# Order of work between latents, expansions, attention and pages in a one-core decoder layer: one change and its time

## The reference

```python
z = h @ lp["w_in"]
c_q, c_kv, k_pe, u = jnp.split(z, [Q_LORA, Q_LORA + KV_LORA, Q_LORA + KV_LORA + ROPE_DIM], axis=-1)
c_q = rms_norm(c_q, lp["q_lora_norm"])
q = (c_q @ lp["w_uq"]).reshape(*c_q.shape[:-1], N_HEADS, NOPE_DIM + ROPE_DIM)
q_nope = rms_norm(q[..., :NOPE_DIM], lp["q_nope_norm"])
q_pe = apply_rope(rms_norm(q[..., NOPE_DIM:], lp["q_pe_norm"]), cos[:, None], sin[:, None])
c_kv = rms_norm(c_kv, lp["kv_norm"])
k_nope = rms_norm((c_kv @ lp["w_uk"]).reshape(*c_kv.shape[:-1], N_HEADS, NOPE_DIM), lp["k_nope_norm"])
v = (c_kv @ lp["w_uv"]).reshape(*c_kv.shape[:-1], N_HEADS, V_HEAD)
# convolution: a causal depthwise window of 31 taps over 512 channels, for prompt and samples
y = lax.conv_general_dilated(xc, lp["conv_w"][:, None, :], (1,), "VALID",
                             dimension_numbers=("NWC", "WIO", "NWC"), feature_group_count=CONV_CH) + lp["conv_b"]
```

## Time and profile before

| what | value |
|---|---|
| median of 3 runs | 1878.46 us (1874.77 to 1879.05) |
| the profiled execution | 1870.42 us |
| its span | 1868.6 us |
| PE busy | 1764.5 us, 94% |
| DVE, ACT, POOL busy | 55%, 28%, 21% |
| mean TensorE clock granted | 0.987 of full speed |

### The profile page before, as it was taken

How to read it: one execution, slowest core, us unless ns; L and a number is a source line. 1 busy time by engine, 2 the same in 40 slices (tenths; PEclk the granted TensorE clock), 3 DMA queues, 4 the chain that set the end, 5 groups by cost and what they waited for, 6 DMA issues and landing times.

```text
span 1868.6 us, 27160 instructions
## 1 busy us (share of the span) xinstructions
PE 1764.5 (94%) x10268; PEld 1558.1 (83%) x10268; DVE 1021.3 (55%) x1659; ACT 529.8 (28%) x1040; POOL 385.6 (21%) x262
## 2 busy tenths in 40 slices
PE   7999798999898999879999999999999999999998
PEld 6999686667887887758788998998998998988886
DVE  5476885545988788766544334344244244244543
ACT  5212255655443444544421111111111111112211
POOL 2205594221545544432210000000000000000000
PEclk9999899999999999999999999999999999999999
DMA  6301000011411222220021111111111111112011
GB/s 197 113 8 40 10 1 1 1 36 37 131 52 52 60 58 56 61 97 1 1 68 46 46 45 45 45 45 45 45 45 45 45 45 45 45 68 76 29 43 41
DMA packets 108947, 91.89 MB, mean 49 GB/s; under 512 B 25571, under 2 KB 97792, under 8 KB 108845
## 3 DMA queue, kind: packets, MB, share of 16 engines
q1 hardware_dynamic: 106851, 89.63, 15.9%
q10 hardware_dynamic: 2002, 1.03, 0.2%
HBM read 84.73 MB, written 6.26 MB: 49 GB/s over the span
## 4 chain that ended last, share of the span: by engine, by line
PE 75%; DVE 12%; POOL 7%; ACT 3%; issue 2%; DMA 1%; ACTq 0%; DVEq 0%; SPq 0%; POOLq 0%
PE ps L1928 21%; PE ps L1930 21%; PE ps L1929 21%; DVE arena L1401 4%; POOL arena L881 2%; POOL stats L750 2%; PE ps L2342 2%; PE ps L2172 2%; DVE arena L1755 2%; PE ps L535 1%; PE ps L1935 1%; PE ps L2129 1%; POOL arena L793 1%; DVE arena L1627 1%; ACT prob_s L1092 1%
## 5 line engine op out<-in xcount | busy, mean ns | idle before, releaser
L1928 PE MATMUL ps<-h_hi,w_hi 128*128 128x384 f32 (+1 forms) x1056 | 345.6, 327 | 2.9 <-POOL h_lo L876 2.9
L1929 PE MATMUL ps<-h_lo,w_hi 128*128 128x384 f32 (+1 forms) x1056 | 345.4, 327 | 0.0
L1930 PE MATMUL ps<-h_hi,w_lo 128*128 128x384 f32 (+1 forms) x1056 | 345.4, 327 | 0.0
L1850 DVE TENSOR_TENSOR gate_s<-gate_s,ps 128x384 f32<-128x384 f32 (+1 forms) x66 | 35.1, 532 | 332.9 <-PE ps L1930 332.9
L881 POOL TENSOR_TENSOR arena<-arena,mhalf 128x32 f32<-128x32 f32 x32 | 173.7, 5429 | 167.5 <-DVE arena L1776 167.5
L1928 PEld LDWEIGHTS ps<-h_hi,w_hi 128*128 128x128 f32 x1056 | 198.5, 188 | 3.4 <-issue 3.1
L1929 PEld LDWEIGHTS ps<-h_lo,w_hi 128*128 128x128 f32 x1056 | 198.5, 188 | 0.5
L1930 PEld LDWEIGHTS ps<-h_hi,w_lo 128*128 128x128 f32 x1056 | 198.5, 188 | 0.0
L1862 DVE TENSOR_TENSOR arena<-arena,ps 128x512 f32<-128x512 f32 x187 | 128.4, 687 | 123.8 <-PE ps L1930 109.6
L529 POOL TENSOR_TENSOR stats<-stats,mhalf 128x1 f32<-128x1 f32 (+1 forms) x18 | 9.8, 543 | 883.1 <-DVE stats L519 883.1
L1928 PE MATMUL ps<-cw_hi,pT_hi 128*128 128x288 f32 x512 | 161.8, 316 | 6.6 <-DVE pT_lo L1674 5.0
(11 more groups left out here) (324 smaller groups left out, 3572.5 us busy)
## 6 DMA issues: line engine op xcount, KB each, us to landing
arena<-in_cache_ckv SPq DMA_DIRECT2D x128, 128.0 KB, 2.0
w_raw<-in_w_gate SPq DMA_DIRECT2D x22, 512.0 KB, 4.0
w_raw<-in_w_up SPq DMA_DIRECT2D x22, 512.0 KB, 5.2
arena<-in_x_prompt SPq DMA_DIRECT2D x16, 512.0 KB, 5.4
w_uk<-in_w_down SPq DMA_DIRECT2D x11, 512.0 KB, 3.5
w_uv<-in_w_down SPq DMA_DIRECT2D x11, 512.0 KB, 4.2
gw_raw<-in_w_in SPq DMA_DIRECT2D x8, 512.0 KB, 6.0
w_out<-in_w_out SPq DMA_DIRECT2D x1, 4096.0 KB, 13.3
```

The source lines that it names most:

```text
L1850: ch.link(nc.vector.tensor_tensor(gate_s[:, c], gate_s[:, c], ps[:, 2 * b + 1, 0:n], ALU.mult))
L1928: mm(out, left[0], right[0], start=start, stop=False)
L1929: mm(out, left[0], right[1], start=False, stop=False)
L1930: return mm(out, left[1], right[0], start=False, stop=stop)
```

## The change

- In the latents: the last latent tile goes to banks 0 and 1, and the squares of the last two tiles use banks 4 and 5 as scratch. ACT makes the high part of the key weights ahead of `high_c(NT-2)`, DVE the low part ahead of `latents(NT-1)`; the value weights' parts and the last tile's `high_c` and `low_c` move behind the first tile's squares and sums of the expansion. DVE makes no taps in the last latent step.
- On PE: the first keys wait for the squares of the last latent tile, no longer for its latents; `turn_c(NT-1)` stands behind the first keys; the values of tile 1 stand ahead of the first `turn_qk`.
- The samples' products: POOL makes two in latent step 4 and none in steps 7 and 8, so the latent loop makes 0 to 6 where it made 0 to 7; POOL's loop over the tiles of the expansion makes 7 to 15, product 7+i in tile i. DVE's loop there is unchanged.
- Taps: 2 fewer in the latents, 16 in the attention (4 behind the last wide copy of each pair of heads), 61 in place of 75 in the pages, there from page 7 of each sequence.

```diff
@@ -552,7 +552,7 @@
             return 4 if i == 0 else 0
         X_BANK = [0, 4] + [0] * (NT - 2)
         CONST_BANK, GOUT_BANK, CT_BANK, QT_BANK, Q_BANK, K_BANK, V_BANK, KT_BANK = 6, 6, 6, 0, 2, 4, 5, 6
-        Z_BANK = [4 - 2 * (t % 2) for t in range(NT)]
+        Z_BANK = [4 - 2 * (t % 2) for t in range(TILES)] + [0]
         GLU_BANK = [2 + 2 * (j % 3) for j in range(NU)]
         block = ctx.enter_context(nc.Block())
 
@@ -804,15 +804,17 @@
             pool.wait_ge(s_("hist_ready"), 2)
             for i in range(1, NT):
                 stat_z(i)
-                taps_sample(i - 1)
+                if i <= 4:
+                    taps_sample(i - 1)
+                if 4 <= i <= 6:
+                    taps_sample(i)
                 if i == 3:
                     pool.wait_ge(s_("w_high"), W_HIGH("wq"))
                     nc.gpsimd.tensor_tensor(wq_lo_r, wq_raw, wq_hi, ALU.subtract).then_inc(s_("w_low_pool"), 1)
             for i in range(NT):
                 stat_qk(i)
                 k_rope(i)
-                if i < 4 * CCH - (NT - 1):
-                    taps_sample(NT - 1 + i)
+                taps_sample(NT - 2 + i)
 
             pool.wait_ge(s_("khr_ready"), NT)
             pool.wait_ge(s_("qkv_done"), QKV(TILES, 3))
@@ -821,6 +823,7 @@
                 ch.link(nc.gpsimd.memset(pages[s][:, :, KL:KL + 1], 1.0))
                 nc.gpsimd.memset(pages[s][:, NPAGE, 0:KL], 0.0).then_inc(s_("page_set"), 1)
                 pool.wait_ge(s_("page_set"), s + 1)
+            pool.wait_ge(s_("ys_prod"), 4 * CCH)
             nc.gpsimd.memset(s_self[64:P, :, :, :], NEG).then_inc(s_("self_place"), 1)
             pool.wait_ge(s_("self_place"), 1)
             pool.wait_ge(s_("lat_stored"), 2 * NT * 16)
@@ -993,9 +996,12 @@
                     act.wait_ge(s_("row_sumsq"), NT + i)
                 else:
                     act.wait_ge(s_("hist_ready"), 1)
-                nc.scalar.activation(ps[0:r, 0, 0:QL], ps[0:r, b, 0:QL], ACT.Square, accum_out=st(z)[0:r])
-                nc.scalar.activation(ps[0:r, 1, 0:KL], ps[0:r, b + 1, 0:KL], ACT.Square, accum_out=st(z + 1)[0:r])
-                nc.scalar.activation(ps[0:r, 1, KL:KL + DR], ps[0:r, b + 1, KL:KL + DR], ACT.Square,
+                if i == NT - 2:
+                    act.wait_ge(s_("lat_ready"), i)
+                d = 0 if i < NT - 2 else 4
+                nc.scalar.activation(ps[0:r, d, 0:QL], ps[0:r, b, 0:QL], ACT.Square, accum_out=st(z)[0:r])
+                nc.scalar.activation(ps[0:r, d + 1, 0:KL], ps[0:r, b + 1, 0:KL], ACT.Square, accum_out=st(z + 1)[0:r])
+                nc.scalar.activation(ps[0:r, d + 1, KL:KL + DR], ps[0:r, b + 1, KL:KL + DR], ACT.Square,
                                      accum_out=st(z + 2)[0:r]).then_inc(s_("row_sumsq"), 1)
 
             def high_c(i):
@@ -1005,6 +1011,10 @@
                     src = ps[:, CT_BANK + b, 0:(k1 - k0) * P].rearrange("p (k c) -> p k c", c=P)[:, :, 0:r]
                     last = nc.scalar.activation(cT_hi_r[:, k0:k1, t * P:t * P + r], src, ACT.Copy)
                 last.then_inc(s_("act_high"), 1)
+            def high_kv(hi, w):
+                for k in range(LC):
+                    last = nc.scalar.activation(hi[k], w[:, k, :], ACT.Copy)
+                last.then_inc(s_("w_high"), 1)
             square_z(0)
             act.wait_ge(s_("glu_ready"), NU)
             nc.scalar.activation(glu_s[:, :, :, HIST:HIST + TQ], glu_new.rearrange("p c (b q) -> p c b q", q=TQ), ACT.Copy)\
@@ -1016,18 +1026,13 @@
                 square_z(t)
                 if t == 1:
                     act.wait_ge(s_("unit_done"), NU)
+                if t == NT - 1:
+                    act.wait_ge(s_("wkv_loaded"), 32)
+                    high_kv(wk_hi_r, w_uk)
                 high_c(t - 1)
                 if t == 3:
                     act.wait_ge(s_("wq_loaded"), 16)
                     nc.scalar.activation(wq_hi_r, wq_raw, ACT.Copy).then_inc(s_("w_high"), 1)
-
-            act.wait_ge(s_("z_done"), NT)
-            act.wait_ge(s_("wkv_loaded"), 32)
-            for hi, w in ((wk_hi_r, w_uk), (wv_hi_r, w_uv)):
-                for k in range(LC):
-                    last = nc.scalar.activation(hi[k], w[:, k, :], ACT.Copy)
-                last.then_inc(s_("w_high"), 1)
-            high_c(NT - 1)
 
             def square_qk(i):
                 r = rows_of(SEQ_TILES[i])
@@ -1062,6 +1067,9 @@
             for i in range(NT):
                 square_qk(i)
                 copy_qk(i)
+                if i == 0:
+                    high_kv(wv_hi_r, w_uv)
+                    high_c(NT - 1)
                 if i >= 1:
                     act.wait_ge(s_("qkv_done"), QKV(i, 3))
                     nc.scalar.activation(V[:, SEQ_TILES[i], :], ps[:, V_BANK, :], ACT.Copy).then_inc(s_("v_ready"), 1)
@@ -1497,22 +1505,25 @@
             ch.link(nc.vector.tensor_tensor(gq_col[0:DN, :], gq_col[0:DN, :], gk_col[0:DN, :], ALU.mult))
             ch.link(nc.vector.tensor_scalar(gq_col[0:DN, :], gq_col[0:DN, :], SCALE, None, ALU.mult))
             ch.link(nc.vector.tensor_scalar(g_qpe[:, :], g_qpe[:, :], SCALE, None, ALU.mult))
+            def low_kv(hi, lo, w, name):
+                dve.wait_ge(s_("w_high"), W_HIGH(name))
+                for k in range(LC):
+                    last = nc.vector.tensor_tensor(lo[k], w[:, k, :], hi[k], ALU.subtract)
+                last.then_inc(s_("w_low_dve"), 1)
             taps(2)
             latents(0)
             taps(2)
             for i in range(1, NT):
+                if i == NT - 1:
+                    low_kv(wk_hi, wk_lo_r, w_uk, "wk")
                 latents(i)
                 low_c(i - 1)
-                if i >= 2:
-                    sum_sample(i - 2)
-                taps(2)
-
-            for hi, lo, w, name in ((wk_hi, wk_lo_r, w_uk, "wk"), (wv_hi, wv_lo_r, w_uv, "wv")):
-                dve.wait_ge(s_("w_high"), W_HIGH(name))
-                for k in range(LC):
-                    last = nc.vector.tensor_tensor(lo[k], w[:, k, :], hi[k], ALU.subtract)
-                last.then_inc(s_("w_low_dve"), 1)
-            low_c(NT - 1)
+                if 2 <= i < NT - 1:
+                    sum_sample(i - 2 + (i > 4))
+                if i < NT - 1:
+                    taps(2)
+                if i == 4:
+                    sum_sample(3)
 
             def sums_q(i):
                 r = slice(0, rows_of(SEQ_TILES[i]))
@@ -1556,6 +1567,8 @@
             dve.wait_ge(s_("z_done"), NT)
             sums_q(0)
             sums_k(0)
+            low_kv(wv_hi, wv_lo_r, w_uv, "wv")
+            low_c(NT - 1)
             for i in range(NT):
                 if i >= 1:
                     qT_copy(i - 1)
@@ -1609,6 +1622,7 @@
                 if k >= 1:
                     wide_copy(k - 1)
                 if first:
+                    taps(4)
                     out_rows(2 * (k // TILES) - 2)
                 if k + 1 < STEPS:
                     row_max(0, k + 1)
@@ -1756,7 +1771,7 @@
                         .then_inc(s_("ksum_done"), 1)
                     if prev and g == 4:
                         row_of_max(b - 1, 1 - s)
-                    if g >= (4 if b == 0 else 6 - b % 2):
+                    if g >= 7:
                         taps(1)
                     if b == NSEQ - 1:
                         if g in WO_PAGE.values():
@@ -2077,18 +2092,20 @@
             for i in range(NT):
                 expand_q(i)
                 if i == 0:
-                    turn_c(NT - 1)
-                    pe.wait_ge(s_("lat_ready"), NT)
+                    pe.wait_ge(s_("row_sumsq"), 2 * NT)
                     pe.wait_ge(s_("w_low_dve"), 6)
                 else:
                     pe.wait_ge(s_("qk_copied"), 2 * i)
                 expand_kv(i, K_BANK, wk_hi_r, wk_lo_r)
-                if i >= 1:
+                if i == 0:
+                    turn_c(NT - 1)
+                if i == 1:
+                    pe.wait_ge(s_("w_low_dve"), 7)
+                    expand_kv(i, V_BANK, wv_hi_r, wv_lo_r)
                     turn_qk(i - 1)
-                    if i == 1:
-                        pe.wait_ge(s_("w_low_dve"), 7)
-                    else:
-                        pe.wait_ge(s_("v_ready"), i - 1)
+                if i >= 2:
+                    turn_qk(i - 1)
+                    pe.wait_ge(s_("v_ready"), i - 1)
                     expand_kv(i, V_BANK, wv_hi_r, wv_lo_r)
```

## The result

| | before | after |
|---|---|---|
| median | 1878.76 us (1874.77 to 1879.4, 4 runs) | 1905.09 us (1897.98 to 1909.43, 4 runs) |
| profiled execution | 1870.42, span 1868.6 | 1897.98, span 1896.1 |

The change makes the kernel slower: the ratio is 1.0141, 95% interval 1.0106 to 1.0176. The forecast was 1904.6. Further down, one execution of c_product_between (3009 us) and two of the kernel before (2000 and 3836 us) are left out of ranges and ratios. The two profiled spans differ by 27.5 us.

What follows compares the result with a forecast made beforehand. POOL was full in the expansion, paced at 8.2 us a tile by query statistic, scaling and sums. Terms +32.0, +1.7, 0 and −7.5 gave +26.2: 1896.6, by the median's level 1904.6 us; range 1890 to 1918.

Steps and rivals of the forecast that it cites:

- The products' order: Expansion: DVE waits for POOL's product of the same tile; pace 12.9 us a tile, 4.7 more than 8.21.
- the 12.9 and the 13.4 of the prediction: Expansion pace in us a tile: 12.9 if DVE and POOL no longer stretch each other's instructions, 13.4 if they do.
- The boundary: Latents to expansion: work taken out ahead of the first sums brings the first query statistic from 216.61 to 211.0, gain 5.6.
- The nine tiles: Expansion: from 211.0, tiles at 12.9 us end the last scaling at 325.65 instead of 293.65, +32.0 us.
- The clock at the attention's start: Last turns and scores before the attention: PE runs at a low clock after its idle hole, +1.7 us.
- my last term: Whole kernel: 8.04 us added for the median of the runs lying above the profiled execution.
- The taps in the attention: Attention: sixteen taps, four per pair of heads at 5.1 us, hide in DVE's idle 6.20 us; cost 0.
- the other end: Attention: POOL's splits stretch taps to 1.7 us each, overrunning by 0.6 four times, 2.4 us in all.
- The pages: Page stage: fewer, later taps save 4.3 on the last chunk's wait, 1.7 of clock and 1.5 elsewhere; −7.5 us.
- The dip that I let go with it: Page stage: the low PE clock following the last tap's wait goes too, saving 1.7 us.
- The rivals: Whole kernel: PE slows too (0.10); wait doesn't bite (0.05); loop takes only the 0.9 reduction (0.04); attention taps overrun (0.06).
- rival 1: Expansion: PE slows to at most 15.7 us a tile and sets the pace; 1924 us, likelier 1914; chance 0.10.

Runs made afterwards that it cites:

- c_product_between: Kernel after, with POOL's product of each tile moved between the query statistic and the key statistic; 1879.86 us, ratio 1.0018 to the kernel before.
- a_sum_later: Kernel after, with DVE reducing each samples' product of the expansion a tile later, behind the scaling; 1864.3 us, ratio 0.9926 to the kernel before.
- b_products_only: Kernel before, with only the order of the samples' products and their reductions changed as in the change; 1915.84 us, ratio 1.0205.
- e_boundary_only: Kernel before, with only the boundary changed (last latent tile's banks, key weights split first, turn behind first keys); 1877.74 us, ratio 0.9995.
- d_taps_only: Kernel before, with only the taps moved: four per pair of heads in the attention, the pages' taps from page 7; 1870.97 us, ratio 0.9964.
- d_taps_early_pages: Kernel before, with four taps per pair in the attention, the pages' taps still from page 4, 5 or 6; 1865.25 us, ratio 0.9946.
- f_fill_a: a_sum_later plus twelve unread PE transposes ahead of the last query turns; 1861.73 us, ratio 0.993 to the kernel before.
- f_fill_before: Kernel before plus twelve unread PE transposes ahead of the last query turns; 1876.8 us, ratio 0.9998.
- h_early: a_sum_later with the pages' taps back at page 4, 5 or 6 on; 1860.62 us, ratio 0.9918 to the kernel before.
- h_early_fill: h_early plus twelve unread PE transposes ahead of the last query turns; 1858.33 us, ratio 0.99 to the kernel before.
- h_early_again: h_early unchanged, run once more for the spread of its runs; 1860.44 us, ratio 0.9925 to the kernel before.
- t_six_taps: a_sum_later with six taps instead of four per pair of heads in the attention; 1869.91 us, ratio 0.9959 to the kernel before.

## Why the prediction was right, point by point

The pieces of all profiled executions, in us, carry this part:

| kernel | first statistic | expansions | attention's start | pairs 1 to 4 | pages | rest |
|---|---|---|---|---|---|---|
| before | 216.6 | 77.0 | 43.6 | 106.4 | 377.7 | 1047.2 |
| after | 209.5 | 111.4 | 47.8 | 107.8 | 370.8 | 1048.8 |
| a_sum_later | 210.9 | 75.4 | 53.8 | 107.9 | 373.6 | 1050.5 |
| b_products_only | 215.2 | 111.3 | 50.8 | 109.4 | 379.6 | 1050.3 |
| e_boundary_only | 214.4 | 75.4 | 49.0 | 109.4 | 379.2 | 1050.4 |
| d_taps_only | 216.2 | 74.3 | 51.6 | 107.9 | 369.3 | 1050.3 |
| d_taps_early_pages | 215.0 | 74.4 | 43.9 | 107.8 | 367.3 | 1050.5 |
| c_product_between | 209.7 | 88.8 | 50.6 | 109.3 | 369.8 | 1050.4 |
| f_fill_a | 210.3 | 75.2 | 44.2 | 106.4 | 369.8 | 1050.4 |
| f_fill_before | 215.7 | 74.4 | 47.3 | 109.4 | 379.6 | 1050.4 |
| h_early | 210.7 | 75.3 | 47.1 | 107.9 | 366.2 | 1050.4 |
| h_early_fill | 209.2 | 75.0 | 44.6 | 109.4 | 366.5 | 1050.3 |
| h_early_again | 209.4 | 74.9 | 51.1 | 106.4 | 366.1 | 1050.4 |
| t_six_taps | 210.3 | 75.3 | 47.1 | 121.5 | 367.0 | 1048.9 |

- **The products' order**: right, in mechanism and nearly in size. The pace is 12.51 instead of 12.9. POOL idles 4.8 us a tile, as forecast (about 5); DVE's wait for the product is 5.5 on average, where I had said some 4. Of the terms, POOL's whole tile is 7.72 (I took 7.9), the reduction 0.86 (0.93), the scaling 2.85 (2.9), sums with hops 1.08 (1.2). Each was a little high. For POOL's tile I had counted out only the 0.32 of L760; its copy of the rotary key fell as well, from 0.50 to 0.40, and L759 and L793 by some 0.05 each. What decides between the 12.9 and the 13.4 of the prediction is that the stretched forms went: with DVE idle POOL's L760 on 8 columns takes 0.24 and not 0.56, and with POOL idle DVE's last rotation takes 0.28 and not 0.48. With this the rule of the Trainium skill, page "SBUF — State Buffer", section "Who interferes with whom", agrees.
- **The boundary**: right. The first statistic came at 209.50, not 211.0, but 1.15 of these 1.5 us are the head start of this execution. Counted from DVE's taps of tile 4 the gain is 5.96, where I forecast 5.6. By the same count the seven other kernels with the whole boundary have 35.03 to 35.05 us up to the first statistic, and the three with the old latents and boundary 40.96 to 40.99, as before, so this measure repeats well. The push by the extra product at tile 4 was there: POOL's statistic of tile 5 came 3.3 later by this count, DVE's latents of tile 5 2.3 later and the last latents 1.5 later (I had 3.4, 2.4 and 1.9).
- **The nine tiles**: the last scaling ended at 320.88, not 325.65, +27.2 instead of +32.0. The 4.8 are 2.1 by the second tile's sums (221.5 instead of 223.6: 1.5 by the first statistic and 0.6 in the first tile, 0.4 of them on POOL) and seven tiles of 0.39.
- **The clock at the attention's start** (+1.7): this term failed. It measured +4.2, and the runs give its reason no support. A fixed dip added to a clean stretch can't be told: the column "attention's start" runs from 43.6 to 53.8 us over kernels in which that stretch holds the same work, and the profiled execution of before was the lowest of all. The 4.2 is a difference between two single executions, well inside that spread; what the change itself adds there stays open. That profile also had the lowest rest, 1047.2, and the lowest value between pairs 1 and 4, 106.4; on the other hand its expansions, 77.0, were 1.6 to 2.7 us above those of every kernel with that loop, the dip of the earlier trace rows. Such differences between executions are what my last term, 8.04 for the level of the median, stood for, and it did its work: the medians' difference, 26.3, is near that of the profiles, 27.5.
- **The taps in the attention** (0): right, by luck in its reason. I compared 5.1 us with the 6.20 of idle time and set the other end at 1.7 a tap. Two of the four places have POOL's splits beside them and the taps took 7.32, or 1.83 each: past that end. They were hidden all the same, because the earlier trace rows shows a hole up to the row scaling, and the deadline is later, at PE's next need of it. From the kernel before alone, the 1.97 us that DVE idles behind the scaling could have been added to the 6.20.
- **The pages** (−7.5): right, −6.9 between the two profiles. The last tap's wait went as said (5.1 to 0.8); the waits at the rotary turns gave 2.3 and those at the products 0.5, where I had 1.5 for both. The dip that I let go with it (1.7) came back elsewhere: over the last sequence, 806 to 848 us, the granted clock was 0.92, where before it was 1.00 over 782 to 822. Alone, the taps gave 6.6 us. I had counted three places where PE waits for DVE and missed the largest, 11.8 at L2332; it stayed (12.1), so the sum did not suffer.
- **The rivals**: none came. PE's clock fell often in its holes (0.88 over the 58 us, 0.75 to 0.91 tile by tile), but the pace stayed at 12.51 to 12.54: the slow stretches found room in PE's holes, the reason for which I gave rival 1 only 0.10.

That the sum came out within 0.5 us of the median is luck: errors of opposite sign met, −4.8 in the expansions with the boundary, and +2.5, +1.4, +0.6 and +1.6 in the terms behind them. The method was good to some 5 us, not to 0.5.

## What to carry to other kernels

Where a product is made at the end of one engine's step and consumed ahead of another engine's critical work, one step of distance hides it and none puts the whole step into the loop: ask of each reader whether its producer stands before or behind the work that the reader's queue feeds. A hole is measured up to the next engine's need, not to the next instruction of the idle engine, and fill is sized with its neighbours running. When a change is a bundle, put the parts on the old kernel one by one: here one place in the order carried a loss of some 38 to 41 us, and the rest was worth a gain of 13. And check that the parts add up to the bundle: here two taps were in none of them. To compare two profiles piece by piece, count from an instant just ahead of the first changed instruction, since the executions differ before it too (here by up to 1.9 us).

## What the runs showed of the hardware

- The granted clock behind a thin stretch of PE differs from execution to execution of the same instructions: between the end of the expansions and the first pair's end, 43.9 us at a mean clock of 0.96 and 51.6 at 0.77. The Trainium skill, page "TensorE: Matmul & The Clock Gate", Part 1, says that the activity window runs free of the program, so that the number of slow matmuls at a kernel's start varies from run to run. The traces agree in the spread, here in the middle of a kernel; whether a free-running window makes it, no run here shows. The spread is not small for such comparisons: this one place has 10 us between its extremes, 0.5% of 1870. The mean clocks of a_sum_later's six runs, 0.979 to 0.988, go with times of 1873.75 to 1857.96.
- DVE's taps beside POOL's splits come out unequal: in the kernel after most of the 120 taps take 1.28 us, the longest 3.37. It stretches both sides: beside the four taps a POOL split of 96x512 took 2.26 us, where the same one took 1.27 in the kernel before, and in t_six_taps one of 96x1024 took 3.35 where its neighbour took 2.36, while the six taps took 12.83 instead of the 7.88 of six with POOL idle.
